# Attention of a hybrid encoder: P V in two passes instead of three, with the softmax denominators summed beside the exponential

## The chip, the cores and the metric

The kernel runs on one core of a Trainium2 chip. The metric is the device time of one execution in microseconds (us), lower is better. A core has a matrix engine (TensorE, PE), VectorE (DVE), ScalarE (ACT), GpSimd (POOL) and SyncE (SP), each with its own queue of instructions that runs in order; they wait for each other by semaphores. On-chip memory is SBUF (128 partitions) and PSUM (8 banks of 128 x 512 float32), into which TensorE writes.

## The reference

Two layers of an encoder over 1024 tokens of width 1024, in float32. Of a layer, the part that matters here is attention with 8 heads:

```
scale = 1.0 / math.sqrt(QK_HEAD_DIM)              # 96 = 64 (nope) + 32 (rope)
sc = einsum('bqhd,bkhd->bhqk', qn_b, k_nope) + einsum('bqhr,bkr->bhqk', qr_b, k_rope)
w = jax.nn.softmax(sc * scale, axis=-1)
o = einsum('bhqk,bkhd->bqhd', w, v)               # v: 1024 tokens x 64 per head
...
mix = concat([group_rms_norm(attn, g_attn_out, N_HEADS), group_rms_norm(conv, ...)])
x = x + rms_norm(mix @ w_out, g_post_mix)
```

Each head's output is divided by its root mean square over its 64 channels (plus 1e-6 under the root). A factor common to all 64 channels of a token cancels in that norm but for the 1e-6. So the kernel doesn't divide by the softmax's denominator: it takes the norm of the unnormalized output, with the 1e-6 scaled by the squared denominator. An MLP and a gated embedding follow; the change leaves them alone.

## The kernel before, in words

Float32 products are made exact enough by splitting each operand into a high and a low part of a reduced 32-bit type (fp32r). A product is three matmuls (`split_product`): high x high, high x low, low x high. ScalarE writes the high part (a copy, L1189), VectorE the low part (a subtraction, L1559 or L1777).

A layer runs: input projection with latents and convolution, attention, output projection ("mix"), MLP, gate. Every engine's program is written out by hand; the order in the source is the order on the engine, but for loops (`Fori`) over groups of the MLP and, before, over the two middle pairs of heads.

**A head of attention** has eight steps s = 0..7, one for each block of 128 queries. In step s TensorE does, in this order (`head`, L963):
- `transposes` of P of block s: eight 128 x 128 blocks, from `pr` into banks 4 and 5 (L926)
- `scores` of block s + 2 (queries x keys, 1024 keys) into banks 0 to 3
- a piece for the next head: K and V projection in s0 and s1 (`keys_and_values`), the transposition of V from channels to tokens in s3 (`values_by_token`, L886), Q projection in s4 and s5 (`queries`)
- in s3 and s7 a `variances` matmul pair (L961): s7 that of the first half (t = 0, queries 0 to 511) of this head, s3 that of the second half (t = 1) of the head before
- `values`: half of the P V of two earlier blocks, 256 queries wide, accumulated over the 8 blocks of keys into bank 6 (t = 0) or 7 (t = 1).

V's stationary operand is 128 columns wide: 64 columns of V and 64 columns of ones (in the low part zeros). So half of the output rows is the head's output and the other half holds the denominators, each repeated 64 times.

Beside it, VectorE takes in step s the low part of the transposed P (`ptl`, L1777), the maximum of each row of scores of block s + 2 (L1767), and from it the exponential's bias `nm` (L1770). ScalarE makes the high part of the transposed P (`pth`, L1189) and then the exponential of block s + 1 (L1361). TensorE's next transpositions wait for that exponential. In s2 (second half of the head before) and s6 (first half of this head), after the exponential, ScalarE squares all 128 rows of the output bank (`sq`, L1380) and copies the output's 64 rows to `of` (`outputs`, L1375); both wait for semaphore o_lo, which says that VectorE has taken the low part of the preceding output (`yl`, L1559, by `low_of_output`), since `of` is one buffer. After the variance ScalarE takes logarithm and exponential (`output_factor`, L1231 and L1233), VectorE multiplies (`output`, in s0 and s4), ScalarE takes the high part `yh`, and VectorE the low part `yl` in s1 and s5.

SyncE issues all transfers. `load_head(h)` brings a head's projection weights into `stage`; ScalarE and VectorE split them in s6 of head h - 2. `store_attention` (L687) writes `yh` and `yl` to DRAM. During the last head ten loads of 512 KB (L706, L707) bring five of the eight chunks of the mix operand back, then come two weight units (L609), two more chunks, and the last one when all is stored.

## Time and profile before

| | us |
|---|---|
| median of 3 runs | 2951.22 (2950.4 to 2951.98) |
| profiled execution | 2950.78, its span 2948.7 |
| TensorE matmul busy | 2879.2 (98%) |
| VectorE busy | 1708.4 (58%) |
| ScalarE busy | 1193.3 (40%) |
| GpSimd busy | 112.1 (4%) |
| mean TensorE clock granted | 0.992 of full |

Busy time of an engine is the union of its instructions' spans. Matmuls overlap in the records, so the time that one costs is the distance between the starts of two. The profile's lines of the kernel after the change have other numbers.

### The profile page before, as it was taken

The page shows a single profiled execution, that of the slowest core. Times are in us where ns is not written, and L with a number is a line of the kernel's source. Part 1 is how long each engine was busy: PE and PEld are TensorE (multiplying, and loading weights), DVE is VectorE, ACT ScalarE, POOL GpSimd, SP SyncE. Part 2 cuts the span into 40 slices and gives each one's busy share as a digit, 9 for nine tenths or more (in the row PEclk, how much of TensorE's full clock was granted, in tenths as well). Part 3 has the DMA queues.
Part 4 walks back from the last instruction along what each step waited for, and adds up shares of the span by engine and source line. Part 5 has one row for each costly group of instructions (what it writes and reads, how often), then busy time and mean ns, then how long its engine had stood idle before and what let it go on. Part 6 is the DMA issues. An engine that isn't in the chain of part 4 may idle for free.

```text
span 2948.7 us, 36240 instructions
## 1 busy us (share of the span) xinstructions
PE 2879.2 (98%) x13824; PEld 2397.8 (81%) x13824; DVE 1708.4 (58%) x2360; ACT 1193.3 (40%) x1793; POOL 112.1 (4%) x78
## 2 busy tenths in 40 slices
PE   6999999999999999999999999999999999999996
PEld 5877888888888888888887788888888888888885
DVE  4356677546445444458765567674654444544786
ACT  4335666545112112126643366665532211211473
POOL 0221000000000000000013200000000000000000
PEclk9999999999999999999999999999999999999998
DMA  4120000432111111113232100006211111111231
GB/s 145 58 76 34 21 24 19 154 129 79 30 56 53 47 43 57 43 57 100 100 107 78 48 27 24 15 19 228 79 51 57 43 45 55 54 46 43 72 100 72
DMA packets 60995, 190.57 MB, mean 65 GB/s; under 512 B 6752, under 2 KB 6752, under 8 KB 60896
## 3 DMA queue, kind: packets, MB, share of 16 engines
q1 hardware_dynamic: 60896, 189.22, 19.2%
q8 instruction: 66, 1.08, 0.2%
q14 instruction: 33, 0.27, 0.0%
HBM read 164.03 MB, written 25.17 MB: 64 GB/s over the span
## 4 chain that ended last, share of the span: by engine, by line
PE 94%; DVE 3%; ACT 1%; DMA 1%; issue 1%; POOL 1%; SPq 0%; DVEq 0%; ACTq 0%
PE ps L754 29%; PE ps L756 29%; PE ps L755 29%; PE ps L926 4%; PE ps L886 1%; PE ps L961 1%; DVE ptl L1777 0%; PE ps L800 0%; PE ps L822 0%; ACT pth L1189 0%; PE ps L793 0%; DVE hl L1559 0%; DVE wl L1559 0%; DMA xf<-x_in 0%; POOL cv L1972 0%
## 5 line engine op out<-in xcount | busy, mean ns | idle before, releaser
L754 PE MATMUL ps<-hh,wh 128*128 128x512 f32 x2192 | 872.0, 398 | 30.9 <-DVE wl L1559 24.1
L755 PE MATMUL ps<-hl,wh 128*128 128x512 f32 x2192 | 857.2, 391 | 0.0
L756 PE MATMUL ps<-hh,wl 128*128 128x512 f32 x2192 | 857.0, 391 | 0.0
L754 PEld LDWEIGHTS ps<-hh,wh 128*128 128x128 f32 x2192 | 414.1, 189 | 126.1 <-issue 27.5
L755 PEld LDWEIGHTS ps<-hl,wh 128*128 128x128 f32 x2192 | 414.2, 189 | 93.6 <-issue 8.2
L756 PEld LDWEIGHTS ps<-hh,wl 128*128 128x128 f32 x2192 | 413.9, 189 | 86.9
L1189 ACT ACTIVATE wh<-raw 128x1024 fp32r<-128x1024 f32 x244 | 254.7, 1055 | 380.1 <-PE ps L756 369.9
L754 PE MATMUL ps<-gh,wh 128*128 128x512 f32 x1024 | 398.5, 389 | 0.0
L755 PE MATMUL ps<-gl,wh 128*128 128x512 f32 x1024 | 398.4, 389 | 0.0
L756 PE MATMUL ps<-gh,wl 128*128 128x512 f32 x1024 | 398.4, 389 | 0.0
L1899 DVE TENSOR_TENSOR xf<-xf,ps 128x512 f32<-128x512 f32 x464 | 310.7, 684 | 146.1 <-PE ps L756 145.5
L1515 ACT ACTIVATE gh<-stage 128x512 fp32r<-128x512 f32 x128 | 80.6, 629 | 715.8 <-DVE stage L1882 715.8
L1559 DVE TENSOR_TENSOR wl<-raw,wh 128x1024 fp32r<-128x1024 f32 x244 | 302.2, 1248 | 108.7 <-ACT wh L1189 107.8
L1882 DVE SCALAR_TENSOR_TENSOR stage<-ps,rpre 128x512 f32<-128x512 f32 x128 | 88.5, 691 | 378.8 <-PE ps L756 374.1
L1777 DVE TENSOR_TENSOR ptl<-ps,pth 128x512 fp32r<-128x512 f32 x256 | 164.9, 685 | 120.7 <-ACT pth L1189 120.1
L754 PEld LDWEIGHTS ps<-gh,wh 128*128 128x128 f32 x1024 | 192.2, 188 | 40.3 <-DVE gl L1559 0.5
L756 PEld LDWEIGHTS ps<-gh,wl 128*128 128x128 f32 x1024 | 192.2, 188 | 39.9
L755 PEld LDWEIGHTS ps<-gl,wh 128*128 128x128 f32 x1024 | 192.2, 188 | 39.8
L1559 DVE TENSOR_TENSOR gl<-stage,gh 128x512 fp32r<-128x512 f32 x128 | 88.6, 692 | 129.3 <-ACT stage L1516 129.2
L1189 ACT ACTIVATE pth<-ps 128x512 fp32r<-128x512 f32 x256 | 138.9, 593 | 52.9 <-PE ps L926 52.3
L754 PE MATMUL ps<-pth,vh 128*128 128x256 f32 x512 | 156.7, 306 | 1.1 <-DVE ptl L1777 1.1
L1767 DVE TENSOR_REDUCE mx<-ps 128x1 f32<-128x1024 f32 x128 | 155.4, 1214 | 2.4 <-PE ps L756 2.4
(135 smaller groups left out, 3294.4 us busy)
## 6 DMA issues: line engine op xcount, KB each, us to landing
raw<-w_units SPq DMA_DIRECT2D x240, 512.0 KB, 3.2
hh<-mix_hi SPq DMA_DIRECT2D x16, 512.0 KB, 6.4
hl<-mix_lo SPq DMA_DIRECT2D x16, 512.0 KB, 7.3
stage<-w_head SPq DMA_DIRECT2D x16, 320.0 KB, 3.0
xf<-x_in SPq DMA_DIRECT2D x4, 1024.0 KB, 9.0
mix_hi<-cyh SPq DMA_DIRECT2D x8, 512.0 KB, 2.7
mix_lo<-cyl SPq DMA_DIRECT2D x8, 512.0 KB, 3.6
mix_hi<-yh SPq DMA_DIRECT2D x32, 128.0 KB, 2.3
```

Of the source, the lines that this page charges most:

```text
L754: nc.tensor.matmul(dst, ah, bh, start=start, stop=False)
L755: nc.tensor.matmul(dst, ah, bl, start=False, stop=False)
L756: return nc.tensor.matmul(dst, al, bh, start=False, stop=stop)
L886: last = nc.tensor.matmul(ps[:, bank, c * V_DIM:(c + 1) * V_DIM], accy[:, c // 4, (c % 4) * P:(c % 4 + 1) * P], cst[:, 0, V_DIM:P], start= ...
L926: last = nc.tensor.transpose(ps[:, 4 + b, c * P:(c + 1) * P], pr[:, s % 2, (4 * b + c) * P:(4 * b + c + 1) * P], ident)
L1189: return nc.scalar.activation(dst, src, ACT.Copy, **more)
L1515: nc.scalar.activation(gh[:, i, hs(b)], stage[:, hs(1)], ACT.Square).then_inc(up_hi, 1)
L1559: return V.tensor_tensor(dst, whole, high.bitcast(f32), ALU.subtract)
L1767: V.reduce_max(mx[:, s % 2:s % 2 + 1], ps[:, 2 * (s % 2):2 * (s % 2) + 2, :].rearrange("p b n -> p (b n)"), AX.X).then_inc(s_max, 1)
L1777: V.tensor_tensor(ptl[at], ps[:, 4 + b, :].rearrange("p (c q) -> p c q", c=4), pth[at].bitcast(f32), ALU.subtract).then_inc(t_lo, 1)
L1882: V.scalar_tensor_tensor(stage[:, hs(1)], ps[:, 2 * b + i, :], 0.0, rpre[:, t, :], ALU.max, ALU.mult).then_inc(up_v, 1)
L1899: V.tensor_tensor(f, f, ps[:, 4 + m % banks, :], ALU.add).then_inc(down_add, 1)
```

## The change

1. V's high and low part stand side by side in one tile, with zeros ahead of them: `vv` = [0 | high | low], 3 x 64 columns per block of keys. P V takes two matmuls for each block: pth against columns 64 to 191 (high | low), ptl against columns 0 to 127 (0 | high). Half of the output rows then holds the sum of the terms with V's high part, the other half the term pth x low. ScalarE copies that second half to `of`, and VectorE adds the first (`output_sum`, new).
2. The denominators are no longer a result of P V. The exponential writes the sum of its row as a second output (`den`), GpSimd squares four columns of it at a time (128 x 4), and SyncE moves them in two transfers (`spread_sums`): to a row of 512 in DRAM (`sums`), and from there to 64 partitions of `sq`. ScalarE squares `of` into the other 64 (`output_squares`, new). The variance matmul reads both as before.
3. V's change from channels to tokens is the transpose form of the matmul, on the 64 partitions that hold V.
4. The query product carries the factor -scale, so that the row's minimum is the exponential's bias without a second instruction.
5. The loop over the middle pairs of heads is written out; the transfers' order on SyncE is another.

```
-            vh = sb("vh", [P, 8, 3 * V_DIM], f32r, att)
-            vl = sb("vl", [P, 8, 3 * V_DIM], f32r, att)
+            vv = sb("vv", [P, 2, 8, 3 * V_DIM], f32r, att)
...
+                def spread_sums(h, t):
+                    O = (L * HEADS + h) * 2 + t
+                    sp.wait_ge(den_sq, O + 1)
+                    sp.dma_start(sums[O].rearrange("(s q) -> q s", q=P), den2[:, h % 2, 4 * t:4 * t + 4], allow_slow_non_contiguous=True).then_inc(den_out, 16)
+                    sp.wait_ge(den_out, 16 * O + 16)
+                    if O:
+                        sp.wait_ge(o_ln, O)
+                    sp.dma_start(sq[rows(1 - h % 2), 0, :], sums[O:O + 1].partition_broadcast(V_DIM)).then_inc(den_in, 16)
...
-                with sp.Fori(1, PAIRS - 1) as j:
+                for j in range(1, PAIRS - 1):
+                    spread_sums(2 * j, 0)
+                    store_attention(j - 1, 1, 1)
                     load_head(2 * j + 2)
-                    store_attention(j - 1, 1, 1)
+                    spread_sums(2 * j, 1)
                     store_attention(j, 0, 0)
+                    spread_sums(2 * j + 1, 0)
+                    store_attention(j, 0, 1)
                     load_head(2 * j + 3)
-                    store_attention(j, 0, 1)
+                    spread_sums(2 * j + 1, 1)
                     store_attention(j, 1, 0)
+                spread_sums(HEADS - 2, 0)
                 store_attention(PAIRS - 2, 1, 1)
+                spread_sums(HEADS - 2, 1)
                 store_attention(PAIRS - 1, 0, 0)
+                spread_sums(HEADS - 1, 0)
+                spread_sums(HEADS - 1, 1)
...
                     for c in range(STEPS):
-                        last = nc.tensor.matmul(ps[:, bank, c * V_DIM:(c + 1) * V_DIM],
-                                                accy[:, c // 4, (c % 4) * P:(c % 4 + 1) * P], cst[:, 0, V_DIM:P],
-                                                start=True, stop=True)
+                        last = nc.tensor.transpose(ps[:, bank, c * V_DIM:(c + 1) * V_DIM],
+                                                   accy[V_DIM:P, c // 4, (c % 4) * P:(c % 4 + 1) * P], cst[V_DIM:P, 0, V_DIM:P])
...
-                        last = split_product(dst, vh[:, c, a * V_DIM:a * V_DIM + P], vl[:, c, a * V_DIM:a * V_DIM + P],
-                                             pth[:, G % 2, c, :], ptl[:, G % 2, c, :], c == 0, c == 7)
+                        nc.tensor.matmul(dst, vv[:, a, c, V_DIM:3 * V_DIM], pth[:, G % 2, c, :], start=c == 0, stop=False)
+                        last = nc.tensor.matmul(dst, vv[:, a, c, 0:2 * V_DIM], ptl[:, G % 2, c, :], start=False, stop=c == 7)
...
                 def variances(h, a, t):
-                    pe.wait_ge(o_copy, (L * HEADS + h) * 2 + t + 1)
+                    O = (L * HEADS + h) * 2 + t
+                    pe.wait_ge(o_sq, O + 1)
+                    pe.wait_ge(den_in, 16 * O + 16)
...
                 def exponentials(h, s):
-                    act.wait_ge(s_neg, step(L, h, s) + 1)
+                    act.wait_ge(s_least, step(L, h, s) + 1)
+                    if s % 4 == 0 and (L or h >= 2):
+                        act.wait_ge(den_sq, (L * HEADS + h - 2) * 2 + s // 4 + 1)
                     nc.scalar.activation(pr[:, s % 2, :], ...,
-                                         ACT.Exp, bias=nm[:, s % 2:s % 2 + 1], scale=SCALE).then_inc(s_exp, 1)
+                                         ACT.Exp, bias=nm[:, s % 2:s % 2 + 1], scale=-1.0,
+                                         accum_out=den[:, h % 2, s:s + 1]).then_inc(s_exp, 1)
...
                     act.wait_ge(pv_out, 2 * O + 2)
                     act.wait_ge(o_lo, O + 1)
-                    nc.scalar.activation(sq[:, 0, :], ps[:, 6 + t, :], ACT.Square).then_inc(o_sq, 1)
-                    copy(of[rows(a), :], ps[rows(a), 6 + t, :]).then_inc(o_copy, 1)
+                    copy(of[rows(a), :], ps[rows(1 - a), 6 + t, :]).then_inc(o_copy, 1)
+
+                def output_squares(h, a, t):
+                    O = (L * HEADS + h) * 2 + t
+                    act.wait_ge(o_sum, O + 1)
+                    nc.scalar.activation(sq[rows(a), 0, :], of[rows(a), :], ACT.Square).then_inc(o_sq, 1)
...
+                        if s == 2 and not first:
+                            outputs(h - 1, 1 - a, 1)
+                        if s == 6:
+                            outputs(h, a, 0)
                         high_of_transposed(h, s, first)
...
                             if s == 2:
-                                outputs(h - 1, 1 - a, 1)
+                                output_squares(h - 1, 1 - a, 1)
...
                         if s == 6:
-                            outputs(h, a, 0)
+                            output_squares(h, a, 0)
...
-                    V.tensor_tensor((tmp, xacc)[t][:, :], ps[:, bank, :], tab[:, hs(t)], ALU.mult).then_inc(q_f, 1)
+                    V.scalar_tensor_tensor((tmp, xacc)[t][:, :], ps[:, bank, :], -SCALE, tab[:, hs(t)], ALU.mult, ALU.mult).then_inc(q_f, 1)
...
-                    V.reduce_max(mx[:, s % 2:s % 2 + 1], ...).then_inc(s_max, 1)
-                    dve.wait_ge(s_max, S + 1)
-                    V.tensor_scalar(nm[:, s % 2:s % 2 + 1], mx[:, s % 2:s % 2 + 1], -SCALE, None, ALU.mult).then_inc(s_neg, 1)
+                    V.tensor_reduce(nm[:, s % 2:s % 2 + 1], ..., AX.X, ALU.min).then_inc(s_least, 1)
...
+                def output_sum(h, a, t):
+                    dve.wait_ge(o_copy, (L * HEADS + h) * 2 + t + 1)
+                    V.tensor_tensor(of[rows(a), :], of[rows(a), :], ps[rows(a), 6 + t, :], ALU.add).then_inc(o_sum, 1)
...
                         low_of_transposed(h, s)
+                        if s == 2 and not first:
+                            output_sum(h - 1, 1 - a, 1)
+                        if s == 6:
+                            output_sum(h, a, 0)
...
+                for h in range(HEADS):
+                    for t in range(2):
+                        O = (L * HEADS + h) * 2 + t
+                        pool.wait_ge(s_exp, step(L, h, 4 * t + 3) + 1)
+                        if O >= 4:
+                            pool.wait_ge(den_out, 16 * O - 48)
+                        part = (slice(None), h % 2, slice(4 * t, 4 * t + 4))
+                        nc.gpsimd.tensor_tensor(den2[part], den[part], den[part], ALU.mult).then_inc(den_sq, 1)
```

On ScalarE, from the end of s0 to s2 of the second head. Before (yh and of: the output; pth: transposed P; pr: its exponential; accy and kh: V and K of the next head):

```order
L1189 ACTIVATE yh<-of 64x512 [waits mix_stored,o_y]
L1189 ACTIVATE pth<-ps 128x4x128 [waits t_out] x2
L1361 ACTIVATE pr<-ps,nm 128x1024 [waits s_neg]
L1189 ACTIVATE accy<-ps 128x512 [waits kv_out]
L1189 ACTIVATE kh<-ps 64x512
L1189 ACTIVATE pth<-ps 128x4x128 [waits pv_out,t_out]
L1189 ACTIVATE pth<-ps 128x4x128 [waits t_out]
L1361 ACTIVATE pr<-ps,nm 128x1024 [waits s_neg]
L1380 ACTIVATE sq<-ps 128x512 [waits o_lo,pv_out]
L1189 ACTIVATE of<-ps 64x512
```

The same place after:

```order
L1217 ACTIVATE yh<-of 64x512 [waits mix_stored,o_y]
L1217 ACTIVATE pth<-ps 128x4x128 [waits t_out] x2
L1391 ACTIVATE pr,den<-ps,nm 128x1024 [waits s_least]
L1217 ACTIVATE accy<-ps 128x512 [waits kv_out]
L1217 ACTIVATE kh<-ps 64x512
L1217 ACTIVATE of<-ps 64x512 [waits o_lo,pv_out]
L1217 ACTIVATE pth<-ps 128x4x128 [waits pv_out,t_out]
L1217 ACTIVATE pth<-ps 128x4x128 [waits t_out]
L1391 ACTIVATE pr,den<-ps,nm 128x1024 [waits s_least]
L1417 ACTIVATE sq<-of 64x512 [waits o_sum]
```

The copy to `of`, with its waits for pv_out and o_lo, now stands ahead of s2's two copies to pth and its exponential; the square stands behind them, with a wait for the sum on VectorE.

On SyncE, in the loop over the middle pairs, ahead of the load of head 2j + 3's weights (`stage`), before (the ISA rows are semaphore waits against a register):

```order
L685 ISA
L687 ISA [waits o_lo]
L687 DMA mix_hi<-yh 64x512
L687 DMA mix_lo<-yl 64x512
L620 REGISTER_ALU
L621 ISA [waits stage_lo]
L621 DMA stage<-w_head 128x640
```

The same place after, first time through (`sums` and `sq` are the two transfers of `spread_sums`):

```order
L692 DMA mix_hi<-yh 64x512 [waits o_lo]
L692 DMA mix_lo<-yl 64x512
L699 DMA sums<-den 128x4x1 [waits den_sq]
L703 DMA sq<-sums 64x512 [waits o_ln,den_out]
L692 DMA mix_hi<-yh 64x512 [waits o_lo]
L692 DMA mix_lo<-yl 64x512
L626 DMA stage<-w_head 128x640 [waits stage_lo]
```

The load stood behind the store of the first output half of head 2j; now it stands behind that of the second half, and behind transfers of head 2j + 1.

On SyncE, during the last head, ahead of the ten mix loads (`hh<-mix_hi`, `hl<-mix_lo`), before:

```order
L687 DMA mix_hi<-yh 64x512 [waits o_lo]
L687 DMA mix_lo<-yl 64x512
L687 DMA mix_hi<-yh 64x512 [waits o_lo]
L687 DMA mix_lo<-yl 64x512
L706 DMA hh<-mix_hi 128x1024 [waits mix_stored,q_out]
L707 DMA hl<-mix_lo 128x1024
```

And after:

```order
L692 DMA mix_hi<-yh 64x512 [waits o_lo]
L692 DMA mix_lo<-yl 64x512
L699 DMA sums<-den 128x4x1 [waits den_sq]
L703 DMA sq<-sums 64x512 [waits o_ln,den_out]
L699 DMA sums<-den 128x4x1 [waits den_sq]
L703 DMA sq<-sums 64x512 [waits o_ln,den_out]
L733 DMA hh<-mix_hi 128x1024 [waits mix_stored,q_out]
L734 DMA hl<-mix_lo 128x1024
```

Both spreads of the last head now stand ahead of the first mix load; the second of them waits for the squares of its last four blocks (den_sq) and for the logarithm of the half before (o_ln).

## Rows read from the trace of the kernel before

**Rows 1.** Page, part 4: shares of the chain that ended last, by engine.

```profile
PE 94%; DVE 3%; ACT 1%; DMA 1%; issue 1%; POOL 1%; SPq 0%; DVEq 0%; ACTq 0%
```

**Rows 2.** Chain of waits, fifth and sixth head: start us, us, engine tile line.

```profile
434.50 1.99 PE ps L886 x16
...
444.57 0.87 PE ps L926 x8
...
450.30 0.87 PE ps L926 x8
...
458.52 0.87 PE ps L926 x8
...
463.57 0.87 PE ps L926 x8
...
468.63 0.87 PE ps L926 x8
472.31 0.45 PE ps L926 x4
...
474.83 1.99 PE ps L886 x16
...
539.11 0.87 PE ps L926 x8
```

**Rows 3.** TensorE timeline, inside a P V: start us, us, instruction [idle before].

```profile
530.00 0.28 PE L754 MATMUL ps<-pth,vh 128*128 128x256 f32 x1
530.12 0.28 PE L755 MATMUL ps<-ptl,vh 128*128 128x256 f32 x1
```

**Rows 4.** ScalarE timeline, s1 and the start of s2.

```profile
464.74 0.63 ACT L1189 ACTIVATE yh<-of 64x512 fp32r<-64x512 f32 x1 [1.49 <-DVE of L1783]
465.28 1.05 ACT L1189 ACTIVATE pth<-ps 128x512 fp32r<-128x512 f32 x2
466.23 1.10 ACT L1361 ACTIVATE pr<-ps,nm 128x1024 f32<-128x1024 f32 x1
467.23 0.60 ACT L1189 ACTIVATE accy<-ps 128x512 f32<-128x512 f32 x1
467.73 0.58 ACT L1189 ACTIVATE kh<-ps 64x512 fp32r<-64x512 f32 x1
469.10 1.09 ACT L1189 ACTIVATE pth<-ps 128x512 fp32r<-128x512 f32 x2 [0.80 <-PE ps L926]
```

**Rows 5.** VectorE timeline: s5, then s1.

```profile
450.23 0.69 DVE L1559 TENSOR_TENSOR yl<-of,yh 64x512 fp32r<-64x512 f32 x1
...
468.34 0.15 DVE L1770 TENSOR_SCALAR nm<-mx 128x1 f32<-128x1 f32 x1
...
469.04 0.67 DVE L1559 TENSOR_TENSOR yl<-of,yh 64x512 fp32r<-64x512 f32 x1
```

**Rows 6.** SyncE timeline: weights of a later head; first of the ten mix loads.

```profile
471.29 0.35 SPq L621 DMA_DIRECT2D stage<-w_head  x1
...
550.83 0.35 SPq L706 DMA_DIRECT2D hh<-mix_hi  x1
```

**Rows 7.** Page, part 6: DMA issues, KB each, us to landing.

```profile
stage<-w_head SPq DMA_DIRECT2D x16, 320.0 KB, 3.0
```

**Rows 8.** Stretches: length, busy PE PEld DVE ACT POOL, PEclk, DMA share, GB/s.

```profile
550.00:568.00 18.00, 17.04 (x119) 15.03 (x118) 12.80 (x21) 14.23 (x22) 0.00 (x0) 1.00 0.89 334
240.00:244.00 4.00, 4.00 (x10) 3.05 (x10) 4.00 (x7) 3.06 (x6) 0.25 (x1) 0.50 0.00 0
```

**Rows 9.** Page, part 3: DMA queue: packets, MB, share of 16 engines.

```profile
q1 hardware_dynamic: 60896, 189.22, 19.2%
```

**Rows 10.** ScalarE and TensorE timelines, end of attention: last weight unit, last variance.

```profile
571.71 1.06 ACT L1189 ACTIVATE wh<-raw 128x1024 fp32r<-128x1024 f32 x1 [1.23 <-DMA raw<-w_units]
...
577.56 1.12 PE L961 MATMUL ps<-sq,cst 128*128 128x512 f32 x2 [1.70 <-ACT of L1189]
```

**Rows 11.** TensorE timeline, last product ahead of attention.

```profile
239.58 0.80 PE L754 MATMUL ps<-hh,wh 128*128 128x512 f32 x1 [3.41 <-DVE hl L1559]
```

63 lines of the change are left out of this document (37 added, 26 removed).

## The prediction

> **What bounds the kernel now.** I read the page's busy lines and the chain of waits first. The reader sees TensorE with 94% of the chain [rows 1], so a matmul taken away counts, unless something else then ends last. Second, the chain through one steady head of attention [rows 2]. A head has eight steps, s0 to s7, and each begins with eight transpositions; the starts of these give the steps' lengths: s5 5.73 us (s4 is like it), s6 and s7 8.22 together (3.68 and 4.54, since s6 holds what s2 holds), s0 5.05, s1 5.06, s2 3.68, and s3, which also holds the V transposition and a variance, the rest. From one V transposition to the next a head takes 474.83 - 434.50 = 40.33 us. Third, the timelines of ScalarE, VectorE and SyncE over the same stretch [rows 4 to 6]: these engines are not the bound, but TensorE waits for them at each step, and the change puts their instructions in another order. Times are counted from one profiled execution of 2950.8 us; the median of the runs is 0.4 us more.
>
> **What goes away on TensorE.** A step of P V issues 12 matmuls of 256 columns, one each 0.118 us [rows 3]; after it 8: 4 x 0.118 = 0.475 us per step. The V transposition takes 1.99 us per head, 16 records [rows 2]. In the transpose form it is 8 of 128x64; I price them as the eight 128x128 transpositions, 0.87 us [rows 2], bounds half of that and 1.99 (nothing saved). Saved: 1.12. Up to the start of a layer's last head (T0 = 539.11 [rows 2]) stand 54 steps of P V and 8 transpositions of V: 54 x 0.475 + 8 x 1.12 = **34.6 us per layer**. Had all else stayed hidden, the ten remaining steps of P V would bring 4.7 more per layer; they are part of the last head, which is worked out by itself below.
>
> **What the moved copy costs.** `of<-ps` of the last output stood behind the exponential of s2 and s6; now it stands ahead of `pth<-ps` there, and it still waits for o_lo, that is for the preceding output's `yl<-of,yh` on VectorE, the last thing VectorE does in s1 and s5. Behind it on ScalarE are two copies to pth and the exponential, and TensorE's next transpositions wait for that exponential.
>
> s2. In s1 the K and V product ends 3.66 us after the step's start in both kernels, since P V comes after it. `yh<-of` of s0 starts 6.22 us after s0's start [rows 4]; s0 shrinks to 4.575, so that is 1.65 into s1. From there by the pitches of [rows 4]: pth at 2.18, exponential 3.13, accy 4.13, kh 4.63 to 5.21; on VectorE kl 5.25, yl 5.85 to 6.52 (before, it ended 6.14 into s1 [rows 5, 2]: 469.04 + 0.67 - 463.57). s1 is now 4.58 long, so o_lo comes 1.94 into s2: copy at 1.98, pth 2.46, exponential 3.43 to 4.55, and s3 starts at 4.60 instead of 3.20: **1.40 us** lost. Before, pth stood at 0.47 into s2 [rows 4], free of it.
>
> s3. ScalarE's next instruction, the square, waits for the new sum `of<-of,ps`, which VectorE can only start after s2's two ptl (3.09 to 4.30 into s2) and which then takes 0.7. So the square runs from 5.02 to 5.55 into s2, and s3's pth starts 0.95 instead of 0.47 us into s3. ptl comes as much later, and the V transposition waits for ptl, since it overwrites the bank that ptl reads: **0.48**.
>
> s6. yl ends 6.35 us after s5's start [rows 5, 2], that is 1.10 into s6 once s5 is 5.255: copy, pth at 1.61, exponential 2.58 to 3.70, s7 at 3.75 instead of 3.20: **0.55**.
>
> Heads 2 to 5 also lose on the weights of the head after next. load_head now stands behind the store that waits for this same yl. From yl's end to the issue were 1.58 us [rows 5, 6], landing takes 3.0 [rows 7]: 5.7 into s6, where ScalarE wants it at 4.7. ScalarE stands there for 1.0 us, with s7's pth and the first exponential of the next head queued behind it: split to 6.4, pth to 7.3, exponential to 8.5, and s0 starts at 8.5 instead of 7.8: **0.7**.
>
> Six heads (1 to 6) lose 2.43 and four of them 0.7: **17.4 us per layer**. The head's own gain of 4.9 is thus half eaten.
>
> **The running sum in the exponential.** The trace shows no exponential with a second output. Bounds: nothing, and a small instruction more, such as VectorE's 128x1 one of 0.15 us [rows 5]. It lies three times per head on the path above, five times in the last head. I take 0.08: **1.8 us per layer**, ends 0 and 3.4. GpSimd's 128x4 squares, `nm` without its second instruction (0.15 us less on VectorE), the scaled query product and the unrolled loop lie beside other work: nothing, bounds -1 and +2 in all.
>
> **The end of a layer's attention.** Before, SyncE issues the ten mix loads from 550.83 on, 11.7 us after T0 [rows 6]; they are 5.24 MB and end near 566.3, 15.5 us after the first issue (18 us at 334 GB/s are 6.0 MB, which are these, one store of 0.26 and one unit of 0.52 [rows 8]). TensorE needs them at 572.3. Now both transfers of head 7's second half stand ahead of them, and these need head 7's last exponential and the logarithm of its first half. I walked the last head, which has no pieces of a next head in it, with the same pitches and waits, in us after T0. s1 starts at 3.2, s2 at 6.9 (its exponential stands behind `yh<-of`, 0.5 late), s3 at 11.1 (the wait of s2, 1.0 here), s4 at 15.1, s5 at 18.3, s6 at 22.0 (as s2). In s5 and s6 ScalarE and VectorE also split a weight unit each time (1.0 and 1.15 us), so yl ends at 23.5, the last exponential at 26.2, and the logarithm at 29.8. The column of sums goes out as 512 pieces of 4 bytes, 32 per engine; lower bound 2.3 us (the small stores), upper that plus 32 x 0.149 us, the mean time of a packet (19.2% of 16 x 2948.7 us over 60,896 [rows 9]) = 7. I take 4.5. It is issued at 26.6 and lands at 31.2; then the spread is issued, then at 31.9 the first mix load, and by the same 15.5 us the ten have landed at **47.4**. TensorE is through with P V at 33 and has nothing else to do.
>
> Two weight units come behind them in the same queue, with a store of 0.26 MB: 1.31 MB at 0.4 MB per us, 50.6. From the second unit's landing to the last variance the chain was 571.71 to 577.56 [rows 10] and gets 0.75 longer by the sum on VectorE: 6.6. The last variance starts at **57.2 after T0; it was 38.45** (577.56 - 539.11): 18.8 lost. All that follows keeps its distance from it.
>
> TensorE idles 14 and then 4 us there. Behind 3.41 us of idleness [rows 11] the granted clock is 0.50, which is 1.2 of 2.4 GHz, from 240 to 244, with 10 matmuls of 512 columns in these 4 us [rows 8], where at full clock there are 17 or 18 (0.23 us each). Half of what runs at 1.2 GHz is lost: for some 5 us of it I add 2.5 us (bounds 1 and 4): **21.3 us per layer**.
>
> The Trainium skill, "DMA: Bandwidth & Descriptors", section "Rules for kernel authors", says that a strided last dimension becomes one descriptor per element, and advises against it. That is my count of 512; no row of this trace has such a transfer. The same section would overlap a DMA by issuing it early and waiting late; the change waits for the first transfer on SyncE itself, ahead of the 5.24 MB.
>
> **Sum.** Per layer -34.6 + 17.4 + 1.8 + 21.3 = +5.9 us, twice +11.8: 2950.8 + 11.8 = 2962.6; I say **2961**. Its own errors: 3 per layer for the heads, 4 for the end, 2 for V: 2943 to 2980.
>
> **Rivals.**
> A. *The moved copy costs nothing*: decided if the preceding yl is ready 0.5 us into s2 and s6. For it: before, nothing on the chain waited there [rows 2]. Against: yl ended 1.1 us into s2 already [rows 5, 2]. Then -34.6 + 21.3 = -13.3 per layer: 2924. Chance 0.13.
> B. *The mix loads are hidden anyway*: -34.6 + 17.4 + 1.8, twice: 2920, chance 0.07; together with A it is the full TensorE gain, 2882, chance 0.03. Against: the loads need 15.5 us and can't be issued before the logarithm of head 7.
> C. *The 4-byte pieces are slow*, 15 us and not 4.5: 10.5 more per layer at the end, 2983. Against: it would be 0.4 us a piece. Chance 0.10.
> D. *The clock also falls inside the heads*, by waits of 1.4 us: some 1.5 us per head, 2980. Times six heads and two layers that is 18. Against: these waits are less than half of the 3.41 us ahead of which the rows show a fallen clock [rows 11]. Chance 0.07.
>
> My own case has 0.60. About 0.2% (6 us) can be told from no change here: of my case 0.42 lie above, 0.15 within, 0.03 below. Faster: 0.13 + 0.10 + 0.03 = 0.26; same 0.15; slower 0.42 + 0.17 = 0.59. The range reaches from B to C: 2920 to 2984.
>
> **What would show it.** Two P V matmuls per chunk, 0.118 us apart, and V in 0.9 us. ScalarE idle ahead of `of<-ps` in s2 until yl; s3's transpositions 4.6 us after s2's; a steady head of 37.8 us, of 38.5 in heads 2 to 5. First mix load some 32 us after the last head's start, TensorE idle 14 us ahead of the first `ps<-hh,wh`, then 4 us ahead of the variance, its clock at half. I am wrong if a head takes 35.4 us, if P V's matmuls get further apart as their number falls, or if the mix loads stand earlier.

## The result

The changed kernel takes 2981.24 us (median of 4 runs, 2981.17 to 2982.68); the kernel before took 2951.39 us beside it (4 runs, 2950.4 to 2951.98). The ratio is 1.0103, with a 95% interval of 1.0085 to 1.012: slower by 30 us. The forecast was 2961, in a range of 2920 to 2984. The profiled execution has a span of 2979.4 us, 30.7 more than before.

TensorE's part of the page, then of the chain that ended last (the shares stand for those in [rows 1]):

```profile
PE 2823.1 (95%) x13184; PEld 2324.1 (78%) x13184; DVE 1712.1 (57%) x2264; ACT 1208.6 (41%) x1921; POOL 118.4 (4%) x108
...
PE 84%; DVE 6%; ACT 5%; DMA 2%; issue 1%; SPq 1%; POOL 0%; ACTq 0%; DVEq 0%
```

TensorE had 94% of the chain and has 84% now. The busy share shows less of it (98% and 95%), since the same matmuls are busy for longer at the half clock: a variance pair that takes 1.13 us elsewhere took 2.08 at the end of attention. The waits of the changed kernel show where the chain leaves TensorE, by engine and line: us in total, times, longest.

```profile
PE ps L952 <- ACT pr L1391: 45.9, 36, 2.7
PE ps L781 <- DMA hl<-mix_lo: 39.6, 2, 19.9
```

So the shape was forecast: TensorE waits for the exponential in the steps with the moved copy, and once per layer for the mix loads.

**Inside a head.** The TensorE timeline of the changed kernel, from s2's transpositions to s3's variance (start us, us, instruction, idle before it and its releaser):

```profile
457.98 1.04 PE L952 MATMUL ps<-cst,pr 128*128 128x128 f32 x8
...
461.08 0.28 PE L980 MATMUL ps<-ptl,vv 128*128 128x256 f32 x1
463.04 1.09 PE L952 MATMUL ps<-cst,pr 128*128 128x128 f32 x8 [1.67 <-ACT pr L1391]
...
465.83 0.71 PE L913 MATMUL ps<-cst,accy 64*128 64x64 f32 x8 [0.31 <-DVE ptl L1816]
466.47 1.13 PE L989 MATMUL ps<-sq,cst 128*128 128x512 f32 x2
```

P V is over at 461.4, and s3 starts 1.67 us later: s2 takes 5.06 us instead of 3.68 [rows 2]. The V transposition now takes 466.47 - 465.83 = 0.64 us instead of 1.99. Why s3 waits stands in ScalarE's and VectorE's timelines:

```profile
458.19 0.59 ACT L1217 ACTIVATE kh<-ps 64x512 fp32r<-64x512 f32 x1
460.18 0.59 ACT L1217 ACTIVATE of<-ps 64x512 f32<-64x512 f32 x1 [1.41 <-DVE yl L1600]
460.80 1.08 ACT L1217 ACTIVATE pth<-ps 128x512 fp32r<-128x512 f32 x2
461.77 1.12 ACT L1391 ACTIVATE pr<-ps,nm 128x1024 f32<-128x1024 f32 x1
462.77 0.21 ACT L1391 ACTIVATION_READ_ACCUMULATOR pr<-ps,nm 128x1 f32 x1
```

```profile
457.48 1.22 DVE L1808 TENSOR_REDUCE nm<-ps 128x1 f32<-128x1024 f32 x1
458.81 0.68 DVE L1600 TENSOR_TENSOR kl<-ps,kh 64x512 fp32r<-64x512 f32 x1
459.42 0.68 DVE L1600 TENSOR_TENSOR yl<-of,yh 64x512 fp32r<-64x512 f32 x1
```

ScalarE stands idle for 1.41 us ahead of the copy until yl is done, and the two copies to pth and the exponential, which TensorE needs, stand behind it. The last of ScalarE's rows is new: each exponential with a sum is followed by a read of the accumulator, 0.2 us. ScalarE's square then waits for VectorE's new sum (462.64 to 463.31), and s3's pth stands behind the square.

The steps of one head, from the starts of their transpositions in TensorE's timelines (s3 to the next s3, us; "sums by matmul" and "third pass" are experiments below):

| | s3 | s4 | s5 | s6 | s7 | s0 | s1 | s2 | head |
|---|---|---|---|---|---|---|---|---|---|
| before | 6.86 | 5.73 | 5.74 | 3.68 | 4.54 | 5.05 | 5.05 | 3.69 | 40.34 |
| changed | 5.62 | 5.26 | 5.28 | 4.20 | 4.32 | 4.65 | 4.57 | 5.06 | 38.96 |
| sums by matmul | 6.44 | 5.26 | 5.27 | 3.21 | 4.71 | 4.60 | 4.58 | 3.21 | 37.28 |
| its third pass | 5.93 | 5.70 | 5.71 | 3.67 | 4.94 | 5.04 | 5.02 | 3.67 | 39.68 |

In the last three rows this is the fifth head, from its s3 on. Heads of two kinds take turns (the output stands in the one or the other half of the partitions): in the head behind it "sums by matmul" has 5.90 for s3, 4.87 for s7, 4.88 for s1 and 3.27 for s2.

**The end of a layer's attention.** The chain that ended last, in order of time (start us, us, what):

```profile
553.61 1.10 ACT pr L1391 x2
554.78 0.21 POOL den L2035
555.00 10.08 DMA sums<-den
565.10 0.46 SPq L703
565.66 0.53 SPq L733
...
572.69 11.90 DMA raw<-w_units
584.61 1.07 ACT wh L1217
...
590.53 0.64 ACT sq L1417
591.21 1.22 PE ps L989
```

The first mix load (SPq L733) is issued at 565.66, 38.0 us after the last head's start at 527.68; before it was 11.7 [rows 6]. The transfer of 512 pieces of 4 bytes alone takes 10.08 us of that. TensorE meanwhile:

```profile
555.88 2.08 PE L989 MATMUL ps<-sq,cst 128*128 128x512 f32 x2
581.58 0.77 PE L781 MATMUL ps<-hh,wh 128*128 128x512 f32 x1 [19.86 <-DMA hl<-mix_lo]
591.21 2.08 PE L989 MATMUL ps<-sq,cst 128*128 128x512 f32 x2 [3.73 <-ACT sq L1417]
```

Stretches of the changed kernel (length, busy time of PE, PEld, DVE, ACT and POOL, granted clock, DMA share, GB/s):

```profile
550.00:566.00 16.00, 8.92 (x50) 7.00 (x50) 7.44 (x10) 7.94 (x14) 0.20 (x1) 0.89 0.07 9
566.00:586.00 20.00, 4.42 (x11) 3.49 (x12) 1.53 (x2) 2.11 (x2) 0.00 (x0) 0.50 0.98 382
586.00:598.00 12.00, 8.28 (x23) 5.64 (x22) 4.50 (x6) 3.69 (x6) 0.00 (x0) 0.70 0.44 163
```

From 550 to 566 the DMA engines move 9 GB/s, while the queue waits for 2 KB for 10 of the 16 us; before they moved 334 there [rows 8]. Then the loads run at 382 GB/s and TensorE has 11 matmuls in 20 us. The last variance starts at 591.21, 63.5 us after the last head's start; before it was 38.6.

**Where the 30.7 us of the spans are.** In layer 0 the last head starts 11.3 us earlier (527.68 against 538.95 in the timelines; the chain of [rows 2] has 539.11, as it puts the start of such a step 0.16 us later) and the last variance 13.65 later (591.21 against 577.56 [rows 10]): the end of attention costs 24.9. From there to layer 1's second V transposition pass 1146.1 us against 1143.9: 2.2 lost behind the wait at the half clock. In layer 1 the six heads gain 9.0 and the stretch from the last V transposition to the last variance loses 22.2 (62.6 to 84.8), as in layer 0 (22.4), which leaves the last variance 29.1 late; 1.6 more are lost behind it.

### The profile page after: what moved, and what is told of

Its sections match the earlier page's. It is cut to its first block, busy times and chain, and to the rows that moved or that the text cites. A ratio compares the mean times of both kernels' runs of the same rounds, so it can differ in the third digit from the quotient of the medians.

```text
span 2979.4 us, 34455 instructions
## 1 busy us (share of the span) xinstructions
PE 2823.1 (95%) x13184; PEld 2324.1 (78%) x13184; DVE 1712.1 (57%) x2264; ACT 1208.6 (41%) x1921; POOL 118.4 (4%) x108
## 2 busy tenths in 40 slices
DMA packets 80456, 194.90 MB, mean 65 GB/s; under 512 B 24160, under 2 KB 24160, under 8 KB 80352
## 3 DMA queue, kind: packets, MB, share of 16 engines
q1 hardware_dynamic: 80352, 193.49, 20.1%
q8 instruction: 69, 1.13, 0.2%
## 4 chain that ended last, share of the span: by engine, by line
PE 84%; DVE 6%; ACT 5%; DMA 2%; issue 1%; SPq 1%; POOL 0%; ACTq 0%; DVEq 0%
PE ps L781 26%; PE ps L783 26%; PE ps L782 26%; PE ps L952 2%; ACT pth L1217 2%; ACT pr L1391 1%; DVE ptl L1816 1%; PE ps L989 1%; DMA raw<-w_units 1%; PE ps L979 1%; PE ps L980 1%; DVE yl L1600 1%; DMA sums<-den 1%; DVE hl L1600 1%; DVE kl L1600 1%
## 5 line engine op out<-in xcount | busy, mean ns | idle before, releaser
L952 PE MATMUL ps<-cst,pr 128*128 128x128 f32 x1024 | 136.6, 276 | 46.9 <-ACT pr L1391 45.9
L952 PEld LDWEIGHTS ps<-cst,pr 128*128 128x128 f32 x1024 | 113.3, 141 | 58.6 <-ACT pr L1391 57.6
L1808 DVE TENSOR_REDUCE nm<-ps 128x1 f32<-128x1024 f32 x128 | 155.4, 1215 | 2.8 <-PE ps L783 2.4
```

What stands on the lines that cost most here:

```text
L952: last = nc.tensor.transpose(ps[:, 4 + b, c * P:(c + 1) * P], pr[:, s % 2, (4 * b + c) * P:(4 * b + c + 1) * P], ident)
L1808: V.tensor_reduce(nm[:, s % 2:s % 2 + 1], ps[:, 2 * (s % 2):2 * (s % 2) + 2, :].rearrange("p b n -> p (b n)"), AX.X, ALU.min).then_inc(s_l ...
```

## The experiments

The theory: (1) TensorE's savings pay, (2) the copy ahead of the exponential takes part of them back, (3) the queue's wait for small transfers ahead of the mix loads takes the rest and more. The rival: one of (2) and (3) costs little, and something else, such as the running sum or late weights, does the harm. Unless said otherwise an experiment changes the changed kernel. All ratios are to the kernel before (2951 us).

**1. Copy back behind the exponential.** The two `of<-ps` copies stand where they stood, VectorE's sum behind the minimum, the squares in the next step.

```diff
 (ScalarE)            if s == 2 and not first:
-                         outputs(h - 1, 1 - a, 1)     # ahead of high_of_transposed
+                     ... # behind the exponential of the same step
+                     if s == 3 and not first:          # between pth and exponential
+                         output_squares(h - 1, 1 - a, 1)
+                     if s == 7:
+                         output_squares(h, a, 0)
```

Expected:

> The changed kernel with one thing undone: ScalarE's copy to `of` stands behind the exponential of s2 and s6 again, VectorE's sum behind the minimum, and the square one step later, between that step's pth and exponential. Theory (the copy's wait for yl is what costs the heads): s2 falls from 5.06 us to 3.2, s3 from 5.35 to about 5.0; s6 falls from 4.1-4.2 to 3.2 where no weights are late. In heads 2 to 5 the weights are then late in s6, so s6 and s7 together give back only 0.5. Six heads x 2.2, two x 0.9, four x 0.5 and 1 us in the last head: 18 us per layer, 36 in all, 2945 us. Rival (ScalarE's and VectorE's sheer load, with the accumulator read of 0.2 us in every exponential, is what costs, not the place of the copy): the wait only moves to other steps, a head stays near 38.7 us and the time above 2970.

Measured: 2996.63 us, ratio 1.0158 (1.0141 to 1.0175), 15 slower than the changed kernel. s6 and s2 did fall to 3.2 us (440.00 to 443.21, 460.94 to 464.16). But s7 rose to 8.17, and ScalarE's timeline shows why; the last row is from layer 1:

```profile
442.84 0.59 ACT L1217 ACTIVATE of<-ps 64x512 f32<-64x512 f32 x1
445.85 0.74 ACT L1217 ACTIVATE wh<-stage 128x640 fp32r<-128x640 f32 x1 [2.41 <-DMA stage<-w_head]
446.61 1.08 ACT L1217 ACTIVATE pth<-ps 128x512 fp32r<-128x512 f32 x2
447.58 0.62 ACT L1417 ACTIVATE sq<-of 64x512 f32<-64x512 f32 x1
...
1836.34 0.74 ACT L1217 ACTIVATE wh<-stage 128x640 fp32r<-128x640 f32 x1 [10.85 <-DMA stage<-w_head]
```

The head's weights, loaded behind a spread and a store, came 2.41 us late, and my moved square stood behind their split, with TensorE's variance waiting for it (48.3 us in 14 waits, in the trace). Most of the loss lies in layer 1, where s7 takes 17.06 and 15.26 us in two heads: from V to the last head layer 1 takes 271.7 us and layer 0 254.6. The weights of the first of these were issued at 1824.48 and landed 11.9 us later, not 3; what held them up is open. The edit mixed the copy's place with the square's. It settles nothing on (2) by itself; experiment 5 mends it.

**2. Head's weights first in the queue.**

```diff
+                    load_head(2 * j + 2)
                     spread_sums(2 * j, 0)
                     store_attention(j - 1, 1, 1)
-                    load_head(2 * j + 2)
...                 # load_head(2 * j + 3) likewise, ahead of spread_sums(2 * j + 1, 0)
```

> The changed kernel with the two load_head calls of the middle pairs ahead of the stores and spreads again, as before the change. Theory: only head 5 waits visibly for its weights in the changed kernel (s7's transpositions to s0's 5.5 us instead of 4.1 to 4.3), heads 2 to 4 at most 0.25 us each; so 1.8 + 0.7 = 2 to 2.5 us per layer, 4 to 5 in all, 2976.5 us. Rival (my prediction as put: 0.7 in each of four heads): 5.6 us in all, which this can't tell apart by the total, but the four heads' lengths can. Second rival (the weights are not late): 2981.

Measured: 2978.23 us, 1.0092 (1.0075 to 1.0109). 3.0 us gained in two layers, hardly more than the spread of the runs: late weights cost little here, since of the heads 2 to 5 only one, in layer 0, shows a clear wait for them (s7 of 5.46 us, 4.13 here). From the second V transposition to the last head this kernel is 2.1 us shorter in layer 0 and 0.6 longer in layer 1. In layer 1 TensorE's clock fell in two heads (granted 0.58 from 1807 to 1811, behind s2's wait of 1.85 us): their s3 take 6.46 and 6.42 us instead of 5.62. The changed kernel's trace has no such fall in these heads.

**3. Mix loads ahead of the last transfer.** SyncE issues the ten mix loads behind the spread of head 7's first half and sends the second half's sums after them.

```diff
                 spread_sums(HEADS - 1, 0)
-                spread_sums(HEADS - 1, 1)
 ...
                 for c in (4, 7, 0, 1, 2):
                     load_mix(c, mix_in)
                 store_attention(PAIRS - 1, 0, 1)
+                sums_out(HEADS - 1, 1)     # between the two weight units
 ...
+                sums_in(HEADS - 1, 1)      # behind the next four mix loads
```

> The changed kernel with the last spread (second half of head 7) taken behind the ten mix loads: SyncE issues the mix loads behind the first-half spread, then the store, a weight unit, the column of sums, the second unit, the two further chunks, and then the spread to 64 partitions. Theory: the mix loads start about 20.5 us after the last head's start instead of 38.0 and have landed at 36.5; the weight units come right behind; the sums, behind 5 MB in the same queue, land about 38, the spread about 42, the last variance starts 42 to 43 us after the head's start instead of 63.5. 21 us per layer and 1 to 2 of clock: 2981 - 45 = 2936 us. Rival (the two weight units and the split chain behind them set the end, not the mix loads' place): the variance stays beyond 55 and the time above 2960.

Measured: 2967.55 us, 1.0054 (1.0037 to 1.007): 13.7 of the 45 us expected. The first mix matmul came 13.6 us earlier (568.00), but then the variance waited for the denominators, as SyncE's and TensorE's timelines show:

```profile
547.36 0.53 SPq L738 DMA_DIRECT2D hh<-mix_hi  x1
...
555.63 0.59 SPq L698 DMA_DIRECT2D sums<-den  x1
...
575.66 0.47 SPq L709 DMA_DIRECT2D sq<-sums  x1
```

```profile
584.58 2.05 PE L996 MATMUL ps<-sq,cst 128*128 128x512 f32 x2 [10.74 <-DMA sq<-sums]
```

The transfer of 2 KB, issued at 555.63 behind megabytes, landed 20.0 us later, and the spread took 8.8 more. So in one queue the sums lose most of what the loads gain.

**4. The same sums as 128 pieces of 16 bytes.** The layout in DRAM is (q s) instead of (s q); the spread then reads the sums of a half in another order, so the small 1e-6 term gets other tokens' denominators.

```diff
-sp.dma_start(sums[O].rearrange("(s q) -> q s", q=P), den2[...], ...)
+sp.dma_start(sums[O].rearrange("(q s) -> q s", q=P), den2[...], ...)
```

> The changed kernel with the sums written as 128 pieces of 16 bytes instead of 512 of 4 (a different order in the row, so each token's 1e-6 term is scaled by another token's denominator). Theory (the pieces' number sets the 8.7 to 10 us of this transfer): it lands in about 3.5 us; at the end of attention the spread is then bound by the logarithm of head 7's first half, 558.7 instead of 565.1 on the changed kernel's clock, 6.4 us per layer earlier: 2968 us. Rival (the time is the write's fixed cost, or comes from the issue): it still lands in 8 us or more, and the time stays at 2981.

Measured: 2967.83 us, 1.0062 (1.0045 to 1.0078), as the theory said. Issue to landing of this transfer in the changed kernel and in this one (min/median/max of 32, us):

```profile
DMA to landing us min/median/max: 8.3/8.7/11.2
```

```profile
DMA to landing us min/median/max: 1.4/1.5/2.8
```

The same bytes in a quarter of the pieces take 7 us less, and the kernel gains 13.4 us, 6.7 per layer; from the last head's start to the last variance the traces show 6.5 less in layer 0 and 5.7 in layer 1. For the whole of this transfer the prediction took 4.5 us.

**5. Copy back and weights early together.** Edits 1 and 2.

> The changed kernel with two edits together: ScalarE's copy of one half of the head's output stands behind the exponential again (the kernel with that edit alone took 2996.6 us, 15 more than the changed one), and the head's weights are loaded ahead of the stores and of the spread (alone: 2978.2). Theory: the copy ahead of the exponential costs 1.4 to 1.9 us in step 2 and some 0.5 in step 6, and the kernel with the copy put back lost only because its squares then stood behind the split of weights that came 2.4 us late; with the weights early that wait goes, so steps 2 and 6 near 3.3 us each and no ACT wait for the stage buffer, the end of attention unchanged: 2950 to 2965 us. Rival: the squares between the transposed copy and the exponential of the next step cost 0.6 us in each of two steps of a head (14 steps a layer, 17 us in all), and eat the gain: 2975 to 2995 us.

Measured: 2949.93 us, 0.9996 (0.9986 to 1.0005): no difference from before, at the lower end of what the theory said. Against experiment 2, from which only the copy's place (and the square's) differs, it gains 28.3 us, 14.2 per layer: (2) holds. Some 1.6 of the 28.3 are the two falls of the clock in experiment 2, which this kernel's heads don't have. Heads take 36.6 us from V to V instead of 38.5 (means of six in layer 0). The end of attention is as bad as it was: TensorE waits 18.14 us for the mix loads.

**6. Sums by matmul.** As 5, but no denominator goes through DRAM; SyncE's order is that of the kernel before.

```diff
                     pe.wait_ge(o_sq, O + 1)
-                    pe.wait_ge(den_in, 16 * O + 16)
-                    nc.tensor.matmul(ps[:, 6 + t, :], cst[:, 3 + a, :], sq[:, 0, :], start=True, stop=True).then_inc(o_var, 1)
+                    nc.tensor.matmul(ps[:, 6 + t, :], cst[:, 3 + a, :], sq[:, 0, :], start=True, stop=False)
+                    pe.wait_ge(den_sq, O + 1)
+                    for i in range(4):      # eye: identity times 64e-6, bf16; den2: bf16
+                        last = nc.tensor.matmul(ps[:, 6 + t, i * P:(i + 1) * P],
+                                                den2[:, h % 2, 4 * t + i:4 * t + i + 1].to_broadcast([P, P]), eye[:, :],
+                                                start=False, stop=i == 3)
```

> As the kernel with copy back and weights early, but no denominator goes through DRAM: GpSimd squares the four sums, and four matmuls of 128x128 in bf16 (the squared sum of a step spread over the columns, times an identity scaled by 64e-6) add them to the variance in PSUM; SyncE's order is that of the kernel before. Theory: the two DMAs of a spread held back the mix loads and the last variance by some 19 to 25 us a layer, so they come off twice, and 128 added matmuls cost at most 0.1 us each, 10 us in all: 2955 less 44 plus 10, about 2920 us (2900 to 2940), with the first mix matmul within 36 us of the last head's start and the variance behind it at once. Rival: the end of attention is late for another reason (the mix loads' own transfers, or the clock, which the shorter steps let fall): over 2940 us.

Measured: **2908.4 us**, 0.9857 (0.984 to 0.9873). It beats both kernels, by 43 and 73 us. The added matmuls and the end of attention (TensorE):

```profile
441.04 0.39 PE L969 MATMUL ps<-eye,den 128*128 128x128 bf16 x4
441.24 0.36 PE L957 MATMUL ps<-pth,vv 128*128 128x256 f32 x1
...
555.87 1.12 PE L966 MATMUL ps<-sq,cst 128*128 128x512 f32 x2 [1.80 <-ACT sq L1401]
```

Four of them take 0.20 us. The squared sums are rounded to bf16 for them; they enter the result only through the 1e-6 term. SyncE issues the first mix load of layer 0 at 528.38, no matmul waits for the loads any more, and the last variance starts 19.4 us earlier than in experiment 5 (575.23), though each head is 0.5 us longer.

**7. Only the sums by matmul**: the hunk of 6 and weights first in the queue, the copy ahead of the exponential as in the changed kernel.

> The changed kernel with only its denominators moved off the DMA queue (GpSimd squares them, four bf16 matmuls add them to the variance; SyncE's order as in the kernel before); the copy stays ahead of the exponential as in the changed kernel. Theory: against the changed kernel's 2981.2 it wins 20 to 25 us at each layer's end of attention and 1.5 for the one head that waited for its weights, and pays up to 10 us for 128 small matmuls: 2940 us (2930 to 2955). Rival: if the copy's place costs little and the transfers all, this one and the kernel with the copy back differ by under 5 us; by the theory they differ by about 20.

Measured: 2941.06 us, 0.9969 (0.9958 to 0.9981), as forecast. Against experiment 2 it gains 37.2 us by the transfers' removal, with the cost of the 128 small matmuls taken off; against 6 it loses 32.7 us by the place of copy and square. Of these some 1.7 are a fall of the clock in one head of each layer, behind s2's wait of 1.84 us (s3 of 6.75 and 6.79 us, 5.90 in the like heads). (2) and (3) each hold with the other one present or absent.

**8. No running sum.** The exponentials write no sum; a constant of 300 stands in for the denominators.

```diff
-                                         ACT.Exp, bias=nm[...], scale=-1.0, accum_out=den[:, h % 2, s:s + 1])
+                                         ACT.Exp, bias=nm[...], scale=-1.0)
```

> The changed kernel whose exponentials write no running sum; a constant of 300 set once stands in for the denominators (it leaves out their summation, which enters the result only through the 1e-6 term); everything else, transfers too, is the same. Theory: 128 accumulator reads of 0.20 us go and the exponential releases the transposition 0.1 us earlier; the steps in which TensorE waits for the exponential (36 such waits in the changed kernel's trace) shorten by 0.3 us, some others partly: 2968 us (2962 to 2973). Rival: ScalarE has room everywhere but in step 2, so under 4 us: 2977 or more.

Measured: 2978.69 us, 1.0093 (1.0076 to 1.011): 2.5 us, the rival's side, and hardly clear of the runs' spread. The 128 reads are 25.8 us of ScalarE's time, but ScalarE has room for them. In s2 of the head shown above it goes

```profile
460.92 1.08 ACT L1217 ACTIVATE pth<-ps 128x512 fp32r<-128x512 f32 x2
461.90 1.12 ACT L1391 ACTIVATE pr<-ps,nm 128x1024 f32<-128x1024 f32 x1
463.46 0.63 ACT L1416 ACTIVATE sq<-of 64x512 f32<-64x512 f32 x1 [0.45 <-DVE of L1821]
```

The square waits for VectorE with or without the read.

**9. A third pass of P V** on experiment 6: one more matmul per chunk, with the zero block as weights, so that it adds nothing.

```diff
+                        nc.tensor.matmul(dst[0:V_DIM], vv[:, a, c, 0:V_DIM], ptl[:, G % 2, c, :], start=False, stop=False)
                         last = nc.tensor.matmul(dst, vv[:, a, c, 0:2 * V_DIM], ptl[:, G % 2, c, :], start=False, stop=c == 7)
```

> The kernel with sums by matmul (2908.4 us) with a third P V pass of 64x256 per chunk put back, whose weights are the zero block, so that it adds nothing to the result: 512 more matmuls, as many as the kernel before had. Theory: P V pays its whole pitch on TensorE's path, 0.118 us each, of which the prediction counted 54 steps of 0.475 a layer: 2908 plus 51 to 61, 2960 to 2970 us. Rival: in the steps in which the transposition waits for the exponential or for the low part the third pass fills a wait, and 10 us or more of it are hidden: under 2955.

Measured: 2944.39 us, 0.9982 (0.9972 to 0.9991): 36.0 us more, the rival's side. The table of steps shows where 512 x 0.118 = 60.4 us shrink to that: s4, s5, s6, s0, s1 and s2 each get 0.44 to 0.46 us longer, but s7 only 0.23, and s3 gets 0.51 *shorter*. In the heads of the other kind s3 stays at 5.90, s1 gets 0.15 longer and s7 0.22. In experiment 6 the V transposition waits up to 1.1 us for VectorE's ptl; with longer steps that wait is gone (5.5 us in seven heads against 1.4). From the second V transposition to the last head it is 17.1 us more in each layer. VectorE in experiment 6, from s2's minimum to s3's ptl:

```profile
417.67 1.22 DVE L1793 TENSOR_REDUCE nm<-ps 128x1 f32<-128x1024 f32 x1
418.92 0.69 DVE L1806 TENSOR_TENSOR of<-of,ps 64x512 f32<-64x512 f32 x1
419.64 1.29 DVE L1801 TENSOR_TENSOR ptl<-ps,pth 128x512 fp32r<-128x512 f32 x2
```

It has no pause there, and the V transposition starts at 420.99, behind the last of these. In the kernel before, the same ptl stands behind a pause of 1.07 us:

```profile
473.41 1.29 DVE L1777 TENSOR_TENSOR ptl<-ps,pth 128x512 fp32r<-128x512 f32 x2 [1.07 <-ACT pth L1189]
```

**10. V turned by plain matmuls**, on experiment 6.

```diff
-last = nc.tensor.transpose(ps[...], accy[V_DIM:P, ...], cst[V_DIM:P, 0, V_DIM:P])
+last = nc.tensor.matmul(ps[...], accy[:, ...], cst[:, 0, V_DIM:P], start=True, stop=True)
```

> The kernel with sums by matmul with V turned by plain matmuls over 128 partitions, as in the kernel before. Theory: a head's eight take 1.99 us instead of 0.64, 16 heads: 2908 plus 21, 2926 to 2931 us. Rival: the step with V's transposition waits 0.7 us a head for the low part of the transposed anyway, and the next one waits less after a longer step: plus 10 or less, 2918.

Measured: 2930.95 us, 0.993 (0.9913 to 0.9946): 22.6 us more, 1.41 per head. But the heads don't pay alike. Most get 1.15 to 1.3 us longer (37.21 to 38.36), somewhat less than the 1.35 of the instructions. Four of the sixteen get 2.7 longer: in them the clock fell behind the V products, ahead of which TensorE had waited 1.13 us. The row of one, the stretch behind it, and the same stretch of experiment 6:

```profile
428.00 2.00 PE L891 MATMUL ps<-cst,accy 128*128 128x64 f32 x16 [1.13 <-DVE ptl L1802]
```

```profile
430.00:434.00 4.00, 4.00 (x18) 3.03 (x18) 0.69 (x1) 1.81 (x3) 0.00 (x0) 0.57 0.00 0
```

```profile
423.00:427.00 4.00, 4.00 (x27) 3.58 (x27) 1.97 (x4) 3.51 (x6) 0.00 (x0) 1.00 0.01 4
```

Four falls of 1.57 us are 6.3 us; from layer 0's last variance to layer 1's second V transposition this kernel is 1.6 us shorter than experiment 6. Without both, the V term is some 18 us, 1.1 per head.

**11. The variance behind P V of its step**, on experiment 6.

```diff
-                        if s == 3 and not first:
-                            variances(h - 1, 1 - a, 1)
-                        if s == 7:
-                            variances(h, a, 0)
                         if s >= 2:
 ...
                             values(h, a, (s - 2) // 2, s % 2)
 ...
+                        ... # the same four lines here
```

> The kernel with sums by matmul with the variance issued behind P V of its step instead of ahead of it. Theory: TensorE's 9 us of waits for the squares in the trace of that kernel are covered by P V's 0.95 us, so it gains some 4 to 8 us: 2901 to 2905 us. Rival: the logarithm and with it the output's stores come 1 us later and the end of attention, which ends with that chain, gives it back: 2908 or more.

Measured: 2908.84 us, 0.9856 (0.9839 to 0.9872): no gain. The heads are 0.5 us shorter each, and the last variance of layer 0 starts 2.4 us earlier than in experiment 6. But it now ends a longer wait, and the clock is down afterwards; TensorE's row and the stretch of this kernel, then the same stretch of experiment 6:

```profile
553.48 2.08 PE L966 MATMUL ps<-sq,cst 128*128 128x512 f32 x2 [3.66 <-ACT sq L1401]
```

```profile
550.00:560.00 10.00, 6.53 (x17) 4.45 (x18) 2.82 (x4) 3.69 (x6) 0.00 (x0) 0.66 0.35 120
```

```profile
550.00:560.00 10.00, 8.20 (x40) 6.19 (x39) 4.48 (x7) 3.89 (x7) 0.00 (x0) 1.00 0.55 198
```

From the last variance of layer 0 to layer 1's second V transposition this kernel takes 1146.7 us, experiment 6 1143.8: 2.9 us given back, more than was won. It is neither the theory's way nor quite the rival's: the output's chain did not come late, the longer wait cost the clock. Experiment 6 has a fall of the clock there too, an earlier and shorter one: granted 0.57 from 545 to 549, behind a wait of 2.71 us.

## Why the prediction was right in kind and short in size

It said slower, for two reasons, and both were shown. Per layer, in us, its terms; half of what the runs differ by; and what the traces of layer 0 give for the stretch from the second V transposition to the last head's start:

| term | predicted | half of the runs' difference | that stretch of layer 0 |
|---|---|---|---|
| P V, 54 steps x 0.475 | -25.6 | -18.0 (experiment 9) | -17.1 |
| V transposition, 8 x 1.12 | -9.0 | -11.3 (10, with falls of the clock) | -8.3 without two falls of the clock, -11.4 with them |
| moved copy, 6 x 2.43 | +14.6 | +14.2 (5 against 2), +16.3 (7 against 6) | +12.5 (5 against 2) |
| weights, 4 x 0.7 | +2.8 | +1.5 (2) | +2.1 |
| running sum | +1.8 | +1.3 (8) | +0.9 |
| end of attention | +18.8 | | +24.9, behind that stretch |
| clock behind it | +2.5 | | +2.2, behind that stretch |

The halves in the third column contain the last head and every fall of the clock, so they don't add up to a reading of the terms; the last column does. In its stretch lie 53 of the 54 steps, seven of the eight transpositions and 18 of the 23 exponentials, for which the prediction has -14.2 us. The column's first five add up to -9.9, and the two kernels themselves differ by -10.4 (254.48 against 264.90). So the heads gained 4 us less per layer than was forecast, and the end of attention cost 6 more: that is most of the way from the forecast's +5.9 to the 15.9 by which layer 1's second V transposition comes late (1737.30 against 1721.44; the medians give 15 per layer). The rest of the change (the scaled query product, the loop written out) has no experiment of its own; half a microsecond is left for it here.

The measured 2981.2 lies above what the prediction gave as its own errors (2943 to 2980). It is inside the range because that reached to rival C.

**The term that failed is P V.** "A matmul taken away counts": 54 steps at the full 0.475 us. The rate was right (0.118 us apart, before and after), and in the head of the table it holds in six of the eight steps, in the other kind of head in five. But s3 and s7 have another bound, and in the other kind s1 too. s3 holds the V transposition, which waits for VectorE's ptl; VectorE has a sum of 0.69 us more to do there and no pause left (experiment 9), so once all steps around it are shorter that wait grows: in s3 nothing of the 0.475 is won, and in one kind of head 0.5 us is lost. s7 gains half; what bounds it, and s1, was not tested. I had worked out how a wait of s3 grows by the moved copy, and had not asked what it does when P V alone shrinks. The experiment was made without the copy ahead, where these waits are 0.8 us per head instead of 0.4 (11.0 and 5.8 us over 14). In the changed kernel itself the size of this term is thus not measured by itself; but with the 17.1 of the experiment the terms add up to within 0.5 us, and with the forecast's 25 they would miss by more than 7. The head in the table is 1.38 us shorter where 1.8 was forecast for one with late weights (38.5 from 40.33), and it lost only 0.28 on weights (38.68 in experiment 2).

**The moved copy** was right in place and near in sum, but not step by step. s2 loses more than the 1.40: it is 5.06, not 4.60. ScalarE's copy starts 2.20 us into s2, not 1.98; 0.16 of this is that I took the starts of steps from the chain and all else from timelines, which have such a start 0.16 us earlier. pth stands 0.62 behind the copy's start, not 0.48, and the exponential releases TensorE 0.1 later. s6 is 4.20, not 3.75, for the same three reasons. Against that, s3 and s7 give some back: with the copy behind, s3 takes 6.16 and s7 4.44 (experiment 5), with it ahead 5.62 and 4.13 (experiment 2), where a further loss of 0.48 in s3 was forecast. A head of the changed order takes 2.0 us more, not 2.43 (38.68 against 36.71): the errors mostly cancel.

**The end of attention** went as it was walked, in us after the last head's start: the last exponential ended at 27.0 (forecast 26.2), the sums were issued at 27.3 (26.6), landed at 37.4 (31.2), first mix load at 38.0 (31.9), first mix matmul at 53.9 (47.4), last variance at 63.5 (57.2). Of the 6.3 us between 57.2 and 63.5 the transfer of 4-byte pieces is 5.6: 10.08 us where 4.5 was taken, above its upper bound of 7. That bound used the mean time of a packet in [rows 9], which is one of kilobytes; a piece of 4 bytes was dearer, an estimated 0.24 us ((10.08 - 2.3) / 32) instead of 0.149. The Trainium skill, "DMA: Bandwidth & Descriptors", section "Rules for kernel authors", warns of one descriptor per element for such a pattern. The case agrees: 80,352 packets in the queue instead of 60,896 [rows 9], and in experiment 4, with 384 pieces fewer in each of the 32 transfers, 68,064, which is 32 x 384 fewer. Experiment 4 also puts a price on it. Rival C (slow pieces, 15 us) was thus half right. Its 2983 lies near the measured time by luck, since it has the rest of the forecast in it.

**The clock** was taken at 2.5 us per layer. Its cost behind the last wait shows by itself in the 2.2 us between the layers, and experiment 11 shows 2.9 behind a wait of 3.66 us. Rival D, a lower clock inside the heads, did not come in the changed kernel: its waits of 1.67 to 1.85 us in s2 left the eight transpositions behind them at 1.09 us, and from the second head to the seventh the granted clock stayed at 1.00 in both layers. But this was no safe distance. In experiments 2, 3, 4 and 7 it did fall in one or two of these heads, behind waits of 1.84 or 1.85 us in s2, and in four heads of experiment 10 behind a wait of 1.13 us, at 0.8 to 2.3 us a fall. The argument against rival D, that these waits are less than half of 3.41 us, does not hold as a rule; what decides is open.

**The late weights** were found in one head of four, and in layer 0 only; rivals A and B are out by experiments 5 and 6: without the copy ahead the heads are 2 us shorter each, and without the transfers the loads are hidden. Together, with the 9 us that the small matmuls cost (0.27 us in s3 and 0.28 in s7, experiment 6 against 5, times 32), this is the case that A with B forecast as 2882: 2908 - 9 = 2899 measured, and the 15 us that P V gave short of its 51 are most of what lies between.

## What to carry to other kernels

A value that TensorE needs spread over partitions need not go through DRAM: a matmul with a broadcast column as weights and a scaled identity did for a quarter of a microsecond what two transfers did in 13 (8.7 and 4.3), and, more to the point, it left the queue free for the megabytes behind them. Before moving an instruction ahead on an engine, list what it waits for and what stands behind it; here a copy of 0.6 us cost 2 us per head by that. A chain that an instruction joins on a second engine counts too: VectorE's sum of 0.69 us stands where the pause was that shorter steps could have used. And where two kernels differ by a few microseconds, look at the granted clock of every stretch first: a part of the difference can be a fall of the clock in one of them. Lastly, count a saved matmul in full only in the steps where no other engine's result is due within the time saved.

## What the hardware showed that was not expected

- A sum beside an exponential is not free on ScalarE: 128 rows of ACTIVATION_READ_ACCUMULATOR, 202 ns each, 25.8 us of ScalarE's time. Without it the time was 2.5 us less in all.
- 512 pieces of 4 bytes from SBUF to DRAM take 8.3 to 11.2 us, 128 pieces of 16 bytes 1.4 to 2.8, and the former once took 20.0, issued behind ten loads of 0.5 MB.
- Eight transpositions of 64x128 in the transpose form take 0.64 us; as plain fp32 matmuls over 128 partitions they take 1.99.
- A wait of 3.66 or 3.73 us on TensorE is followed by some microseconds at the half clock, which cost 2 to 3 us. Shorter waits can be followed by them too, and need not be: waits of 1.84 and 1.85 us in s2 left the clock up in most heads and were followed by a fall in some (experiments 2 and 7, 0.8 to 0.9 us each), and a wait of 1.13 us with the V products behind it was followed by one in four heads of experiment 10 (1.6 us each).
